# Layer 2's conditioning slabs further apart, rope of queries before the keys, attention earlier in the scan, output matrix from the heads on, half of the Fourier sums

## The reference

```python
mod = silu(c) @ w_ada[li] + b_ada[li]           # six vectors of 1024: shift, scale, gate, twice
m = unpack(modulate(rms_norm(x, n1), sh1, sc1) @ w_in[li])     # qa ka va qh zf zb ih gh uf
att  = head_norm(diff_attend(rope(qa), [ctx_ka, rope(ka)], [ctx_va, va], lam))
rec  = rms_norm(hgrn_scan_forward + hgrn_scan_backward) * silu(gh)
four = fft2(uf, axes=(1, 3), norm='ortho').real @ w_fnet
x = x + g1 * (concat[att, rec, four] @ w_out)
x = x + g2 * conv_ffn(modulate(rms_norm(x, n2), sh2, sc2), w_up, conv_w, conv_b, w_down)
```

## Time and profile before

| | us |
|---|---|
| median of 3 runs (1920.79 to 1933.95) | 1930.21 |
| the profiled execution | 1927.21 |
| its span | 1925.3 |

### The profile page before, as it was taken

The page is one execution under the profiler, slowest core; times in us unless marked ns, Lnnn a source line. Parts: engine busy times, 40 slices in busy tenths (PEclk is TensorE's granted clock), DMA queues, the critical chain, the costliest instruction groups (busy, mean ns, idle before and its releaser), DMA issues.

```text
span 1925.3 us, 27917 instructions
## 1 busy us (share of the span) xinstructions
PE 1823.5 (95%) x11564; PEld 1525.3 (79%) x11564; DVE 1038.1 (54%) x1456; ACT 847.3 (44%) x1223; POOL 91.5 (5%) x171
## 2 busy tenths in 40 slices
PE   5999989899999999998998889999999999999998
PEld 3777866677777778876777779977999979889877
DVE  1333377664544463552646657866556665455475
ACT  2342445433333343354354445554333445565563
POOL 0000012210000000010001200001000010000010
PEclk9999999999999999999998999999999999999999
DMA  9653100125445532235210365543566565555562
GB/s 301 208 181 131 66 1 2 40 92 174 153 155 175 175 102 85 98 115 175 66 44 1 110 196 163 190 164 121 173 182 192 156 192 170 175 165 164 175 122 65
DMA packets 211596, 260.77 MB, mean 135 GB/s; under 512 B 4673, under 2 KB 173299, under 8 KB 211215
## 3 DMA queue, kind: packets, MB, share of 16 engines
q1 hardware_dynamic: 207850, 247.69, 39.7%
q0 software_dynamic: 3232, 11.15, 2.7%
q10 hardware_dynamic: 389, 0.15, 0.0%
HBM read 257.84 MB, written 1.12 MB: 135 GB/s over the span
## 4 chain that ended last, share of the span: by engine, by line
PE 74%; DVE 9%; DMA 6%; ACT 5%; issue 3%; SPq 1%; POOL 1%; DVEq 0%; ACTq 0%; POOLq 0%
PE acc L731 21%; PE acc L733 20%; PE acc L732 20%; DVE weights_low L1908 2%; PE acc L773 2%; ACT weights_high L1464 2%; DMA weights<-in_w_up_dram 2%; DMA weights<-in_w_in_dram 2%; PE acc L985 1%; DVE scratch L2087 1%; PE acc L1209 1%; POOL small L1346 1%; PE acc L714 1%; DMA weights<-in_w_down_dram 1%; DVE scratch L2433 1%
## 5 line engine op out<-in xcount | busy, mean ns | idle before, releaser
L1908 DVE TENSOR_TENSOR weights_low<-weights,weights_high 128x2048 fp32r<-128x2048 f32 (+1 forms) x184 | 416.9, 2269 | 575.1 <-ACT weights_high L1464 575.0
L1464 ACT ACTIVATE weights_high<-weights 128x2048 fp32r<-128x2048 f32 (+1 forms) x184 | 348.3, 1896 | 643.9 <-DMA weights<-in_w_up_dram 193.5
L731 PE MATMUL acc<-normed_t_high,weights_high 128*128 128x256 f32 (+1 forms) x1824 | 580.4, 318 | 15.0 <-DVE weights_low L1908 14.1
L733 PE MATMUL acc<-normed_t_high,weights_low 128*128 128x256 f32 (+1 forms) x1824 | 566.6, 311 | 0.0
L732 PE MATMUL acc<-normed_t_low,weights_high 128*128 128x256 f32 (+1 forms) x1824 | 566.6, 311 | 0.0
L731 PEld LDWEIGHTS acc<-normed_t_high,weights_high 128*128 128x128 f32 x1824 | 348.3, 191 | 43.8 <-DVE weights_low L1908 17.3
L732 PEld LDWEIGHTS acc<-normed_t_low,weights_high 128*128 128x128 f32 x1824 | 345.9, 190 | 24.7 <-issue 4.3
L733 PEld LDWEIGHTS acc<-normed_t_high,weights_low 128*128 128x128 f32 x1824 | 346.0, 190 | 21.1
L731 PE MATMUL acc<-weights_high,normed_t_high 128*128 128x512 f32 (+1 forms) x792 | 309.4, 391 | 6.9 <-DVE normed_t_low L2231 5.8
L733 PE MATMUL acc<-weights_high,normed_t_low 128*128 128x512 f32 (+1 forms) x792 | 305.4, 386 | 0.0
L732 PE MATMUL acc<-weights_low,normed_t_high 128*128 128x512 f32 (+1 forms) x792 | 305.3, 385 | 0.0
(11 more groups left out here) (247 smaller groups left out, 1826.3 us busy)
## 6 DMA issues: line engine op xcount, KB each, us to landing
weights<-in_w_up_dram SPq DMA_DIRECT2D x44, 1024.0 KB, 7.2
weights<-in_attn_w_in_dram SPq DMA_DIRECT2D x40, 1024.0 KB, 5.1
weights<-in_w_ada_dram SPq DMA_DIRECT2D x38, 1024.0 KB, 5.3
weights<-in_conv_w_in_dram SPq DMA_DIRECT2D x32, 1024.0 KB, 5.6
weights<-in_w_in_dram SPq DMA_DIRECT2D x24, 1024.0 KB, 7.4
weights<-in_w_down_dram SPq DMA_DIRECT2D x20, 1024.0 KB, 5.0
arena<-in_w_ada_dram SPq DMA_DIRECT2D x8, 1024.0 KB, 9.7
weights<-in_w_out_dram SPq DMA_DIRECT2D x8, 1024.0 KB, 5.0
```

Source lines behind the costliest of these rows:

```text
L731: pe.matmul(o, ah, bh, start=start, stop=False)
L733: return pe.matmul(o, al, bh, start=False, stop=stop)
L1464: act.activation(hi_slot(n)[:, 0:used], slot(n)[:, 0:used], ACT.Copy).then_inc(hi_in.sem, 1)
L1908: dve.tensor_tensor(slot(n, ring_lo)[:, 0:used], slot(n)[:, 0:used], hi_slot(n)[:, 0:used], ALU.subtract).then_inc(lo_in.sem, 1)
```

## The change

1. **Fourier sums.** The table `dft_seq` has 129 cosine and 127 sine columns in place of 256 and 256. `sequence_sums` makes 256 columns in place of 512. `channel_sums` writes cosine and sine parts beside each other (129 and 127 columns) in place of accumulating them; ScalarE copies them apart, and POOL (`second_half`, new) makes the second half of the positions by subtraction, read backwards, and the first by addition. `fnet_rows` waits for POOL (`four_ready`). The table of constants is 512 columns narrower.
2. **Conditioning slabs of layer 2.** In `w_in` from behind zz (0 and 1), uf and ka 0 to behind va (0 and 1) and ihgh (0 and 1); in `w_up` from behind slabs 0 to 3 to behind slabs 4, 9, 14 and 19. Four fillers are cut: 3 before the second queries' product, 7 before ka, 7 before va, and of 8 in `w_up` 3 stay.
3. **Rope.** The queries' rope, in both layers, stands between uf and ka, on TensorE and on VectorE.
4. **Attention steps.** `weave` divides by `ATT_STEPS = 17`, not by 20.
5. **Output matrix.** `merge_rec` is called inside the first product of `w_out`, when half of the token tiles have had rows 0 to 3. ScalarE and VectorE split rows 0 to 3, then one slab of weights, then rows 4 to 7.

```diff
-    both = np.concatenate([np.cos(ang), np.sin(ang)], axis=1) * scale
+    both = np.concatenate([np.cos(ang)[:, 0:129], np.sin(ang)[:, 1:128]], axis=1) * scale
...
+        ATT_STEPS = 17
...
-                ("w_in", 1): ([(1, n) for n in range(8, 12)], [0, 0, 1, 1, 1, 1]),
-                ("w_up", 1): ([(1, n) for n in range(20, 24)], [1] * 4)}
+                ("w_in", 1): ([(1, n) for n in range(8, 12)], [0] * 7 + [1] * 4),
+                ("w_up", 1): ([(1, n) for n in range(20, 24)], [0, 0, 0, 0, 1] * 4)}
...
-                while done < total * n // HGRN_STEPS:
+                while done < min(total, total * n // ATT_STEPS):
...
-                ("w_in", 1, "qa", 1): 3, ("w_in", 1, "ka", 0): 7, ("w_in", 1, "va", 0): 7, ("w_up", 1, 0, 1): 8,
+                ("w_up", 1, 0, 1): 3,
...
-                heads("ka", slice(0, 512))
...
-                for name, X in (("qa", QA), ("ka", KA)):
-                    for h in range(NH_A):
-                        pe.wait_ge(*taken_after((name, li, h)))
-                        o = open_group(("rot", name, li, h))
-                        pe.matmul(o[:, 0:256], rot, X[:, h, 256:512], start=True, stop=True).then_inc(full, 1)
+                turned_heads("qa", QA)
+                heads("ka", slice(0, 512))
+                turned_heads("ka", KA)
...
-                        last = pe.matmul(o[:, :], UF[:, t, f * P:(f + 1) * P], dft_seq[:, k, :],
+                        last = pe.matmul(o[:, 0:256], UF[:, t, f * P:(f + 1) * P], dft_seq[:, k, :],
...
-                    pe.matmul(o[:, f * 256:(f + 1) * 256], dft_cos, FS[:, f, 0:256], start=True, stop=False)
-                    last = pe.matmul(o[:, f * 256:(f + 1) * 256], dft_sin, FS[:, f, 256:512], start=False, stop=True)
+                    pe.matmul(o[:, f * 256:f * 256 + 129], dft_cos, FS[:, f, 0:129], start=True, stop=True)
+                    last = pe.matmul(o[:, f * 256 + 129:(f + 1) * 256], dft_sin, FS[:, f, 129:256], start=True, stop=True)
...
-                for p in range(2):
-                    pe.wait_ge(*taken_after(("rec", li, p)))
...
-                rows_twice(("w_out", li), live, cols_of)
+                rows_twice(("w_out", li), live, cols_of, lambda: merge_rec(li))
...
+                            if amid is not None and (c, h, n) == (0, 0, len(live) // 2):
+                                amid()
...
+            def second_half(li, s):
+                pool.wait_ge(*taken_after(("f2", li, s)))
+                pool.tensor_tensor(backwards(YT4[:, :, 129:256]), YT4[:, :, 1:128], sines, ALU.subtract).then_inc(pool_step, line.one())
+                pool.wait_ge(pool_step, line.n)
+                pool.tensor_tensor(YT4[:, :, 1:128], YT4[:, :, 1:128], sines, ALU.add).then_inc(four_ready.sem, 1)
...
-                merge_rec(li)
-
                 act.wait_ge(*taken_after(("oT", li, len(att_units(li)) - 1)))
-                for n, r0 in enumerate((0, 4)):
-                    lo = 0 if li == 0 else 256
-                    split_rows(MT[:, :, lo:512], ("w_out", li, 0, r0), n, r0, 4, lo)
+                lo = 0 if li == 0 else 256
+                split_rows(MT[:, :, lo:512], ("w_out", li, 0, 0), 0, 0, 4, lo)
                 act.wait_ge(full, full_after(("E", li, 7, 1, 1)))
-                for n in range(4):
+                split_next()
+                merge_rec(li)
+                split_rows(MT[:, :, lo:512], ("w_out", li, 0, 4), 1, 4, 4, lo)
+                for n in range(3):
...
-                    if (name, h) == ("ka", 1):
-
-                        for name2, X in (("qa", QA), ("ka", KA)):
+                    if (name, h) in (("uf", 0), ("ka", 1)):
+
+                        name2, X = ("qa", QA) if name == "uf" else ("ka", KA)
```

More of the change, by code:

```diff
@@ L377, in program @@
         kd_ready = S("kd_ready", [u for u in UN if u[1] < 6])
+        four_ready = S("transform_ready", [(li, s) for li in range(DEPTH) for s in range(2) if li == 0 or s])
         rec_keys = [(li, t) for li in range(DEPTH) for t in (range(NT) if li == 0 else range(2, NT))]
@@ L643, in weave @@
                 if early_point:
-                    if halves_ and done < total * (n + 1) // HGRN_STEPS:
+                    if halves_ and done < min(total, total * (n + 1) // ATT_STEPS):
                         next(att_steps)
@@ L863, in heads, with turned_heads @@
                         n += 1
+                def turned_heads(name, X):
+                    for h in range(NH_A):
+                        pe.wait_ge(*taken_after((name, li, h)))
+                        o = open_group(("rot", name, li, h))
+                        pe.matmul(o[:, 0:256], rot, X[:, h, 256:512], start=True, stop=True).then_inc(full, 1)
                 def tokens(name, n_of):
@@ L1113, in rows_twice @@
                             if h == 1:
-                                last.then_inc(full, 1)
+                                last.then_inc(full, closed((*name, c, t)))
                         release(last if h == 0 else None)
```

56 lines of the change are left out of this document (32 added, 24 removed).

## The result

The changed kernel takes 1909.86 us (median of 4 runs, 1907.58 to 1911.93), the kernel before 1932.08 in the same series. The recorded ratio of the two kernels is 0.9905, 95% interval 0.9879 to 0.9932; it is an estimate over the runs and not the quotient of the two medians, which is 0.9885. By the ratio the gain is 13 to 23 us and so clear of the noise, but it can't be told whether it is more or less than the 1% on which the forecast had put 0.68. The forecast was 1906, its own range 1899 to 1912. The profiled execution took 1907.58 us, 19.6 less than that of before, with a mean clock of 0.987 against 0.983. The sum of the prediction had said 22.8: the total is nearly right, the terms are not all so.

A forecast was written before the change was run, and what follows sets the result against it. TensorE, busy 95% of the span, was taken as the bound. Terms 4.6 + 17.2 - 1.0 + 2.0 = 22.8 us off 1927.2 gave 1904.4, or 1907.4 by the median; forecast 1906, own range 1899 to 1912, whole range 1893 to 1919.

The forecast's parts named there:

- Half Fourier: Sequence and channel sums: fewer columns gain 4.6 us in layer 1 (floor 3.4), 2.3 in layer 2; POOL passes hidden.
- Projection of layer 2: Slabs, rope and fillers there, with layer 2's Fourier part: 21.9 us go, some returns, net gain 17.2 (bounds 9 to 21).
- the layout's 885 and 907.5: Layer 2's projection, new order laid out: queries' rope matmuls run to 885 us, the keys end at 907.5.
- where the prediction had 8.5: Layer 2's projection, queries' rope behind gate passes: wait 4.1 and filler 4.8 go, less 0.4 of drain, 8.5 us gained.
- The last slab's row: Layer 2's projection: TensorE's 2.5 us wait for this row on ScalarE returns in the new order.
- The 1.5 for the clock: Layer 2's projection: 1.5 us of clock loss charged to the one remaining wait, for the last slab's row.
- Up product: Layer 2, spaced slabs: 17.2 us of waits against 15.4 before; loss of 1.0 taken (5 gained to 8 lost).
- Mixer of layer 1: Attention moved from tail to scan: tail 22.3 to 16.8 us, scan 3.5 longer (bounds 0 and 6.5), net gain 2.0.
- Mixer of layer 2: Attention moved from tail to scan in layer 2: gain and growth taken as equal, 0 us.
- the overlap case: Rival, chance 0.20: extra attention work fits layer 1's scan gaps free, and the last slab's row is ready: 1898 us.
- The case of moved gaps: Rival, chance 0.25: projection's 0.9 us slack breaks, half clock follows three gaps, up product's paired fetches take 9.0: 1915 us.
- The stall at the maximum: Rival, chance 0.05: attention ahead of the scan makes each of 30 steps wait one maximum more, 37 us: 1943 us.

The follow-up runs named there:

- att_alone: Kernel before with the attention at 17 steps in both layers alone, everything else as before: 1934.39 us, ratio 1.0024.
- slabs_in_alone: Kernel before with only the conditioning slabs of layer 2's projection moved behind va and ihgh, rope and fillers kept: 1924.58 us, ratio 0.9982.

## Why the prediction was right, and where not

**Half Fourier, right.** 4.6 us were forecast for layer 1, 4.6 came (4.3 to 5.6 in the other runs), and sequence sums take 1.73 us. In layer 2 1.5 us of the 2.3 show alone. The passes on POOL stayed hidden.

**Projection of layer 2, right but 2 us short.** 17.2 forecast, 19.2 measured, 130 us expected and 127.96 seen. The queries' rope matmuls ended at 888.1 and the keys at 910.3; the layout's 885 and 907.5, with the stage's later start of 2.45 us added, are 887.5 and 910.0. Both rope groups in the chain of after:

```profile
886.39 1.73 PE acc L872 x8
...
910.31 1.73 PE acc L872 x8
```

By cause the terms are less exact than their sum. The early rope was worth 8.3 us, of which 5.9 lie where the prediction had 8.5; slabs gave 3.0, and the cut fillers, which the prediction had spread over its terms as 3.1 and 4.8, gave 5.6. The last slab's row cost 1.9 for 2.5, and the second ihgh product didn't wait at all (0.7 forecast). The 1.5 for the clock was about right: 0.99 over the stage.

**Up product, near in number, not in its terms.** 1.0 lost was forecast, mainly from 17.2 us of waits against 15.4 of before, in which 4.5 were for the clock. TensorE waited 11.5 us in all (9.9 of it for low parts, seven times, 2.8 at most), and the clock was 0.98, hardly won back. In the pair of traces it is 0.2 gained, because the execution of before was one at 0.97; over all fourteen executions it is 1.7 lost with the clock taken out.

**Mixer of layer 1, wrong: this is the step that failed.** "The moved work is some 6 us of TensorE in the scan, which has 14.1 us not busy; I take 3.5" had the work right (7 us) and its cover wrong. The growth was 9.7 in the pair of traces and 9 at equal clock over all runs, beyond the bound of 6.5; in plain lengths against the mean of twelve it is 6.6, just at it. The scan grew by more than the tail gave, 4.6, which the prediction itself had named as a sign of being wrong. TensorE's waits in this stretch, after and then before:

```profile
PE acc L959 <- DVEq L2109: 4.7, 10, 0.8
PE acc L1075 <- ACT mixer_scratch L1713: 3.9, 4, 1.1
...
PE acc L1075 <- DVE mixer_scratch L2205: 1.5, 2, 1.0
PE acc L1008 <- ACT mixer_scratch L1713: 1.4, 1, 1.4
```

```profile
PE acc L953 <- DVEq L2091: 4.9, 9, 1.5
PE acc L1069 <- ACT mixer_scratch L1696: 3.7, 4, 0.9
```

The waits of before are still there in nearly the same sums, but for one of 0.8 us, and two have come in that before doesn't show: 1.5 and 1.4 us, about the 2.8 us by which the time not busy grew. Both stand with the same sums in att_alone. Of the twelve executions at 20 steps none has the second, and three have 0.6 us of the first. So the extra waits come with the moved steps. Why they do was not tested; ScalarE and VectorE have 6.2 and 4.4 us more work in the scan. The tail went from 24.67 to 20.12, 4.6 instead of 5.5. Its end was as foreseen: the seven fillers met half clock. The chain at the end of layer 1's tail:

```profile
363.74 0.74 POOL small L1351
...
364.57 0.38 POOL mixer_scratch L1395
365.00 0.47 PE acc L1093
365.47 5.26 PE acc L717 x14
```

The split that they cover was done at 369.36 (VectorE, from 367.00 on for 2.36 us), and the fillers ran 1 us past it. The output matrix's growth of 1.6 us, the merge's own work, was not priced: the prediction counted it as hidden.

**Mixer of layer 2, gained where nothing was forecast.** 0 forecast, 4.5 gained in the pair of traces. Over all runs scan and tail together are 90.1 to 92.8 us in the seven executions at 20 steps and 87.9 to 89.2 in the five at 17 with the new output order, so 2 to 3 us are the change's and the rest is the long scan of before. The tail lost 3.8 us: 1.7 by the move, which takes 6 of POOL's 13 instructions out of it, and 2.1 by the output order, which then keeps the merge off the path. The prediction had that hiding as 1.6 us, but not that it depends on the move. The scan's length hardly changed, and how shows in the clock: seven executions at 20 steps were granted 0.89 to 0.91 over this scan and took 77.5 to 80.1 us, the six at 17 steps 0.93 to 0.98 and 79.0 to 81.1. With the clock taken out the scan did grow, from 71.4 to 76.8 us. That the added work is why the clock was higher fits the fact that it came in all six, and was not tested by itself; TensorE's time not busy rose here too, from 10.8 to 13.2 us.

**The sum.** Against the forecast's 22.8: scan of layer 1 6.2 worse, output matrix 1.6 and tail 0.9 worse, untouched stages 2.1 worse; projection 2.0 better, mixer of layer 2 4.5, up product 1.2. That makes 19.7. A part of the accuracy was luck: a miss of 6.2 us in one mixer stood against one of 4.5 in the other.

Of the rivals, the overlap case is refuted (the gaps took in nothing, though the late row cost only 1.9). The case of moved gaps is refuted for the projection, whose slack held, and for the up product as well: it wanted fetches of 9.0 us, and the four on the chain there took 5.0 to 6.2. The stall at the maximum isn't there: of its 37 us in 30 places the scan of layer 1 shows 1.5 us in two.

## What to carry to other kernels

Idle time between dependent steps of an engine need not be room for work: in layer 1 7 us put there cost 9, since waits of its own came with it, while in layer 2 the scan's length hardly grew, at a higher granted clock. Where several edits of one stage are made, measure them one by one: here the rope gained 8 us, the slabs 3 with or without it, and cutting the fillers behind both 6. Two edits can also need each other: in layer 2's mixer neither the move nor the output order shows a gain alone, and together they gave 2.5 us. Tune such a number by layer: 20 steps in layer 1 and 17 in layer 2, with the other two edits undone where they gave nothing, took 1898.9 us against the change's 1909.9 (ratios 0.9841 and 0.9905 to the kernel before, whose intervals don't overlap).

## What was unexpected of the hardware

The granted clock of a stretch full of small matmuls differs from one execution to the next, by much: layer 1's scan, the same 947 matmul records, ran at 0.88 in one kernel and 0.97 in another, 128.0 and 119.3 us, though TensorE's longest single wait there was about 1.5 us and its busy share 88% or more. No edit accounts for it: slabs_in_alone, whose program is that of before up to layer 2's projection, had 0.89 and 126.2 us there, before 0.96 and 119.8. It may be much of the 1% by which the times of every kernel here spread, and it is why a stage of a single execution was compared over several: the one of before, at 0.96, has one of the shortest scans of twelve.

A POOL pass of 0.68 us became one of 2.2 to 2.3 beside VectorE's split of two SBUF inputs: in layer 1 in all eight executions that have the pass, in layer 2 in seven of them, and in the eighth, where the split was over before the pass began, it took 0.68.
